# Half-wise state-space results, a setup in 19 beats, a later first batch and a later bonus product in a three-block network kernel

## What is computed

```python
mod = c_act @ w_ada[l] + b_ada[l]
shift, scale, gate = jnp.split(mod, 3, axis=-1)
h = rms_norm(x, norm_g[l]) * (1.0 + scale[:, None, :]) + shift[:, None, :]
u, z_s, q, k, v, z_a = jnp.split(h @ w_in[l], splits, axis=-1)
y_s = s5_mixer(u, ...) * jax.nn.silu(z_s)      # state space, then gelu, then the product with w_glu
y_a = diff_attention(rope(q), rope(k), v, ...) * jax.nn.silu(z_a)
x = x + gate[:, None, :] * (jnp.concatenate([y_s, y_a], axis=-1) @ w_out[l])
```

```python
kk = normalised(k * k_k);  k = k * (1 + (a - 1) * k_a)
y = group_norm(rwkv7_scan(r, decay, k, v, kk, a))
bonus = jnp.sum(r * k * r_k, axis=-1, keepdims=True) * v
return (y + bonus) * g
```

## Time and profile before

| | us |
|---|---|
| median of 3 runs (3295.13 to 3302.15) | 3297.18 |
| the profiled execution | 3302.57 |
| its span in the trace | 3300.5 |
| PE busy | 3008.8 (91%) |
| PE weight loads busy | 2777.6 (84%) |
| DVE busy | 2265.7 (69%) |
| ACT busy | 1621.3 (49%) |
| POOL busy | 324.4 (10%) |

### The profile page before, as it was taken

One profiled execution on the slowest core, in us unless ns is written; L12 is line 12 of the kernel. 1 busy time (PEld: TensorE's weight loads), 2 busy tenths in 40 slices (PEclk: granted clock), 3 DMA queues, 4 the chain that ended last, 5 costly groups with the idle time before them and its releaser, 6 DMA issues.

```text
span 3300.5 us, 60057 instructions
## 1 busy us (share of the span) xinstructions
PE 3008.8 (91%) x24264; PEld 2777.6 (84%) x24264; DVE 2265.7 (69%) x3538; ACT 1621.3 (49%) x2407; POOL 324.4 (10%) x569
## 2 busy tenths in 40 slices
...
GB/s 379 287 243 225 203 209 223 253 198 208 162 155 137 139 147 167 176 179 183 89 112 92 100 108 90 173 130 198 128 171 190 179 192 180 179 187 170 180 147 122
DMA packets 110708, 576.94 MB, mean 175 GB/s; under 512 B 33056, under 2 KB 33088, under 8 KB 46688
## 3 DMA queue, kind: packets, MB, share of 16 engines
...
q10 hardware_dynamic: 576, 3.47, 0.3%
...
## 4 chain that ended last, share of the span: by engine, by line
PE 60%; DVE 24%; ACT 6%; DMA 5%; issue 3%; SPq 1%; POOL 1%; DVEq 0%; ACTq 0%; POOLq 0%
PE acc L911 59%; DVE arena L871 7%; DVE rounded L871 6%; DVE arena L881 3%; ACT arena L908 2%; DVE upper L871 2%; DMA arena<-in_w_ada 2%; ACT rounded L908 2%; DMA arena<-in_w_in 1%; DVE upper L881 1%; ACT upper L908 1%; PE acc L914 1%; SPq L867 1%; DVE rounded L881 1%; DVE arena L877 1%
## 5 line engine op out<-in xcount | busy, mean ns | idle before, releaser
L911 PE MATMUL acc<-rounded 128*128 128x256 f32 x14688 | 1937.1, 291 | 52.6 <-issue 30.4
L911 PEld LDWEIGHTS acc<-rounded 128*128 128x128 f32 x14688 | 1843.6, 196 | 136.1 <-issue 100.3
L871 DVE TENSOR_TENSOR rounded<-arena,rounded 128x1024 fp32r<-128x1024 f32 (+1 forms) x832 | 1005.3, 1208 | 338.8 <-ACT rounded L908 271.0
L908 ACT ACTIVATE rounded<-arena 128x1024 fp32r<-128x1024 f32 (+1 forms) x864 | 883.6, 1023 | 648.7 <-PE acc L911 489.1
L911 PEld LDWEIGHTS acc<-upper_rounded,rounded 128*128 128x128 f32 x4560 | 565.3, 197 | 45.0 <-DVE rounded L871 22.8
L911 PE MATMUL acc<-upper_rounded,rounded 128*128 128x256 f32 x4560 | 573.1, 289 | 23.1 <-DVE rounded L871 20.7
L908 ACT ACTIVATE arena<-arena 128x256 f32<-128x256 f32 (+4 forms) x477 | 253.0, 530 | 306.0 <-DVE arena L871 213.9
L911 PE MATMUL acc<-arena 128*32 128x512 f32 (+8 forms) x1878 | 267.1, 467 | 79.9 <-DMA arena<-in_w_ada 42.7
L871 DVE TENSOR_TENSOR arena<-arena 128x256 f32<-128x256 f32 (+6 forms) x519 | 273.2, 526 | 51.7 <-ACT arena L908 30.1
L911 PEld LDWEIGHTS acc<-arena 128*32 128x32 f32 (+4 forms) x1878 | 122.8, 139 | 143.9 <-DMA arena<-in_w_ada 67.2
L871 DVE TENSOR_TENSOR arena<-acc,arena 128x256 f32<-128x256 f32 (+3 forms) x280 | 119.1, 425 | 178.0 <-PE acc L911 160.3
...
## 6 DMA issues: line engine op xcount, KB each, us to landing
arena<-in_w_in SPq DMA_DIRECT2D x164, 1024.0 KB, 5.0
arena<-in_w_ada SPq DMA_DIRECT2D x88, 1024.0 KB, 5.3
arena<-in_w_up SPq DMA_DIRECT2D x88, 1024.0 KB, 4.8
arena<-in_w_down SPq DMA_DIRECT2D x44, 1024.0 KB, 4.7
arena<-in_w_outa SPq DMA_DIRECT2D x16, 1024.0 KB, 7.3
arena<-in_w_glu SPq DMA_DIRECT2D x16, 1024.0 KB, 5.4
arena<-in_w_outm SPq DMA_DIRECT2D x16, 1024.0 KB, 5.0
arena<-in_w_out SPq DMA_DIRECT2D x16, 1024.0 KB, 4.8
```

Of the source, the lines that this page charges most:

```text
L871: return self.put(self.e and self.e.tensor_tensor(o, a, b, op))
L908: return self.put(self.e and self.e.activation(o, a, f, scale=scale, **kw))
L911: return self.put(self.e and self.e.matmul(o, l, r, start=start, stop=stop, skip_group_check=True))
```

## The change

1. Calls before batch 0: six more in each layer.
2. The results of the state space go out by halves. A new generator `s5_back` waits for batches 7 and 15; for each half it plays `s5_y` (eight writes of half the size), after 14 calls `s5_yr` (POOL waits for them and reads back), after 8 calls the four tiles, each in two beats (`s5_out` with part 0 and 1) three calls apart, and then `part`, 8 calls a tile. The gelu's buffer is a single one, `GS`.
3. `s5_setup` is played in 19 beats. In layer 0 these stay within the same calls as before; in layer 1 each beat has two calls.
4. The recurrent mixer's bonus operand goes to `D2` in place of `RT2`. TensorE's product with it, DVE's product with `v`, the temporary slot and POOL's store belong to step 3, ACT's bias to step 4, and DVE forms `LD` for the exponentials in step 2.
5. `QR`, `QI` (and `SN`) move to the other memory, `XT` to a spare piece of the constants; `upper` grows by 128 columns.

```diff
-IM, QR, QI, R8, ARE, AIM, STP, RE, TH, T1, T2, CO, SI, EM1 = (_c.alloc(64) for _ in range(14))
+IM, R8, ARE, AIM, STP, RE, TH, T1, T2, CO, SI, EM1 = (_c.alloc(64) for _ in range(12))
 P1, P2, PK = (_c.alloc(576) for _ in range(3))
-BC0, BB = _c.alloc(512), _c.alloc(128)
+BC0, GS = _c.alloc(512), _c.alloc(256)
...
+QR, QI = _c.alloc(64), _c.alloc(64)
 KB, VB, PQ = VT_, VT_ + 512, VT_ + 1024
-XT, YT, SN = BB, SI, QR
+XT, YT, SN = CON + CCOL["spare"], SI, QR
...
     def s5(self, l):
-        for i in range(8):
-            self.add("s5_setup", l, i)
-            yield
-            if l:
-                yield
+        for i, parts in enumerate((1, 2, 1, 4, 3, 2, 1, 5)):
+            for part in range(parts):
+                self.add("s5_setup", l, i, part)
+                if l or part == parts - 1:
+                    yield
+                if l:
+                    yield
         self.add("s5_first", l)
         for x in self.s5_prepare(l, 0):
             yield
         for x in self.s5_phases(l, 0):
             yield
         while ("u8", l, 0) not in self.marks:
+            yield
+        for _ in range(6):
             yield
         for b in range(16):
             both = [self.s5_follow(l, b)] + ([self.s5_prepare(l, b + 1)] if b < 15 else [])
...
                     if next(g, self) is self:
                         both.remove(g)
                 yield
-        self.add("s5_y", l)
-        for _ in range(20):
-            yield
-        for j in range(9):
-            self.add("s5_out", l, j)
-            yield
-            yield
-            if j:
-                self.add("part", ("ys", l), j - 1)
-            yield
-            yield
+            self.marks.add(("s5", l, b))
+    def s5_back(self, l):
+        for half in range(2):
+            while ("s5", l, 8 * half + 7) not in self.marks:
+                yield
+            self.add("s5_y", l, half)
+            for _ in range(14):
+                yield
+            self.add("s5_yr", l, half)
+            for _ in range(8):
+                yield
+            for j in range(4 * half, 4 * half + 4):
+                self.add("s5_out", l, j, 0)
+                for _ in range(3):
+                    yield
+                self.add("s5_out", l, j, 1)
+                for _ in range(2):
+                    yield
+                self.add("part", ("ys", l), j)
+                for _ in range(3):
+                    yield
...
-                slot = self.take("rw") if s in (1, 2) else None
+                slot = self.take("rw") if s in (1, 3) else None
...
-                self.bgs += [g5, gm]
+                gy = self.s5_back(0)
+                self.bgs += [g5, gy, gm]
...
-            self.drain(g5)
+            self.drain(g5, gy)
-                g5 = self.s5(1)
-                self.bgs.append(g5)
+                g5, gy = self.s5(1), self.s5_back(1)
+                self.bgs += [g5, gy]
...
-        if s == 2:
+        if s == 3:
             pe.wait_ge("rw_act", ("ld", i))
             pe.wait_ge("rw_dve", ("rk", i))
-            pe.mm(B(4, 0, 256), con("blk"), V(RT2, 256), True, True).then_inc("rw_pe", ("rk", i))
+            pe.mm(B(4, 0, 256), con("blk"), V(D2, 256), True, True).then_inc("rw_pe", ("rk", i))
...
-    def s5_out(l, j):
-        if j < 8:
-            s = TM + 256 * (j % 2)
+    def s5_out(l, j, part):
+        if part == 0:
             act.wait_ge("s5_dve", ("gelu", l, j))
-            act.act(V(s, 256), V(s, 256), ACT.Tanh).then_inc("s5_act", ("gelu", l, j))
+            act.act(V(GS, 256), V(GS, 256), ACT.Tanh).then_inc("s5_act", ("gelu", l, j))
 
...
-        if s == 2:
+        if s == 3:
             bonus[i] = V(TMP + 256 * slot[0], 256)
-        if s == 3:
             act.wait_ge("rw_dve", ("ld2", i))
             act.act(V(RT1, 256), V(CU, 256), ACT.Exp)
             act.act(V(RT2, 256), V(CU, 256), ACT.Exp, scale=-1.0)
             act.act(V(LD, 256), V(LD, 256), ACT.Exp).then_inc("rw_act", ("ex", i))
+        if s == 4:
+            act.wait_ge("rw_dve", ("bo", i))
             act.act(bonus[i], bonus[i], ACT.Identity, bias=par("lnx_b", i)).then_inc("rw_act", ("bo", i))
-        if s == 4:
             act.wait_ge("rw_pe", ("tab", i))
             act.act(V(Q0T, (384, 2), (192, 2), (1, 64)), B(7, 0, (64, 2), (128, 2), (1, 64)), ACT.Copy)
...
+        if i == 3 and part == 0:
             dve.wait_ge("s5_act", ("pk", l))
             dve.copy(V(R8, 64), V(PK + 8, (9, 64)))
             dve.wait_ge("s5_act", ("tanh", l))
             dve.ts(V(T1, 64), V(EM1, 64), -1.0, 1.0, MUL, ADD)
             dve.recip(V(T1, 64), V(T1, 64))
             dve.stt(V(EM1, 64), V(EM1, 64), 2.0, V(T1, 64), MUL, MUL)
-            sin_arg(V(P1, 576), V(TM, 576), V(CC1, 576), con("ph1"), con("ph1r")).then_inc("s5_dve", ("p", l, 0))
-        if i == 4:
-            sin_arg(V(P2, 576), V(TM, 576), V(CC1, 576), con("ph2"), con("ph2r")).then_inc("s5_dve", ("p", l, 1))
-        if i == 5:
+        if i == 3 and part == 1:
+            turns_of(V(CC1, 576), V(TM, 576), con("ph1"))
+        if i == 3 and part == 2:
+            turned(V(P1, 576), V(TM, 576), V(CC1, 576))
+        if i == 3 and part == 3:
+            bounded(V(P1, 576), con("ph1r")).then_inc("s5_dve", ("p", l, 0))
+        if i == 4 and part == 0:
+            turns_of(V(CC1, 576), V(TM, 576), con("ph2"))
+        if i == 4 and part == 1:
+            turned(V(P2, 576), V(TM, 576), V(CC1, 576))
+        if i == 4 and part == 2:
+            bounded(V(P2, 576), con("ph2r")).then_inc("s5_dve", ("p", l, 1))
+        if i == 5 and part == 0:
             sin_arg(V(CO, 64), V(IM, 64), V(T1, 64), 0.25, con("hpi")).then_inc("s5_dve", ("trig", l, 0))
+        if i == 5 and part == 1:
             sin_arg(V(SI, 64), V(IM, 64), V(T1, 64), 0.0, con("zero")).then_inc("s5_dve", ("trig", l, 1))
             dve.ts(V(T2, 64), V(IM, 64), 0.5, None, MUL).then_inc("s5_dve", ("trig", l, 2))
...
-    def s5_out(l, j):
-        if j:
-            i = j - 1
-            s, y = V(TM + 256 * (i % 2), 256), V(U8 + 256 * i, 256)
-        if j < 8:
-            if j == 0:
-                dve.wait_ge("s5_yt", l)
-            yj, sj = V(U8 + 256 * j, 256), V(TM + 256 * (j % 2), 256)
-            dve.stt(yj, V(UT + 256 * j, 256), par("ssm_d", l * 8 + j), yj, MUL, ADD)
+    def s5_out(l, j, part):
+        yj, sj, uj = V(U8 + 256 * j, 256), V(GS, 256), V(UT + 256 * j, 256)
+        if part == 0:
+            dve.wait_ge("s5_yt", (l, j // 4))
+            dve.stt(yj, uj, par("ssm_d", l * 8 + j), yj, MUL, ADD)
             dve.tt(sj, yj, yj, MUL)
             dve.ts(sj, sj, 0.044715 * GELU_C, GELU_C, MUL, ADD)
             dve.tt(sj, sj, yj, MUL).then_inc("s5_dve", ("gelu", l, j))
-        if j:
-            dve.wait_ge("s5_act", ("gelu", l, i))
-            dve.stt(V(UT + 256 * i, 256), s, 1.0, y, ADD, MUL).then_inc("s5_dve", ("out", l, i))
+        else:
+            dve.wait_ge("s5_act", ("gelu", l, j))
+            dve.stt(uj, sj, 1.0, yj, ADD, MUL).then_inc("s5_dve", ("out", l, j))
 
     def att(l, h, i):
         if i == 1:
...
-            dve.stt(V(RT2, 256), V(Rf, 256), par("r_k", i), V(Kf, 256), MUL, MUL).then_inc("rw_dve", ("rk", i))
+            dve.stt(V(D2, 256), V(Rf, 256), par("r_k", i), V(Kf, 256), MUL, MUL).then_inc("rw_dve", ("rk", i))
+            dve.tt(V(LD, 256), V(CU, 256), V(LD, 256), SUB).then_inc("rw_dve", ("ld2", i))
+        if s == 3:
             t = tile_ready(dve, slot)
             dve.wait_ge("rw_pe", ("rk", i))
             dve.tt(V(t, 256), B(4, 0, 256), V(Vf, 256), MUL).then_inc("rw_dve", ("bo", i))
-        if s == 3:
-            dve.tt(V(LD, 256), V(CU, 256), V(LD, 256), SUB).then_inc("rw_dve", ("ld2", i))
             dve.wait_ge("rw_act", ("ex", i))
             dve.tt(V(Rf, 256), V(Rf, 256), V(RT1, 256), MUL)
...
-    def s5_y(l):
-        pool.wait_ge("s5_act", ("y", l, 15))
+    def s5_y(l, half):
+        pool.wait_ge("s5_act", ("y", l, 8 * half + 7))
         for q in range(8):
-            dst = bass.AP(tensor=m.scr_y.tensor, offset=m.scr_y.offset + l * 262144 + q * 32,
-                          ap=[[256, 16], [4096, 64], [1, 32]])
-            pool.dma(dst, V(U8, 64, 32, p0=16 * q, np_=16), "s5_y8", (l, q))
-        pool.wait_ge("s5_y8", (l, 7))
-        pool.dma(V(U8, 8, 256), m.scr_y[l].rearrange("(j p) t -> p j t", p=128), "s5_yt", l)
+            dst = bass.AP(tensor=m.scr_y.tensor, offset=m.scr_y.offset + l * 262144 + half * 131072 + q * 32,
+                          ap=[[256, 16], [4096, 32], [1, 32]])
+            pool.dma(dst, V(U8 + 1024 * half, 32, 32, p0=16 * q, np_=16), f"s5_y8{half}", (l, q))
+    def s5_yr(l, half):
+        pool.wait_ge(f"s5_y8{half}", (l, 7))
+        src = m.scr_y[l, 512 * half:512 * half + 512].rearrange("(j p) t -> p j t", p=128)
+        pool.dma(V(U8 + 1024 * half, 4, 256), src, "s5_yt", (l, half))
...
     def rw(i, s, slot):
-        if s in (1, 2):
```

(5 more changed lines are left out.)

46 lines of the change are left out of this document (29 added, 17 removed).

## The result

The changed kernel's median is 3269.02 us (3267.48 to 3272.13, four runs), the kernel before beside it 3296.15; the ratio is 0.9916, 95% interval 0.9898 to 0.9933. It is faster by 27 us where 57 were forecast. The profiled execution took 3272.13 us with a span of 3270.3, against 3302.57 and 3300.5.

A forecast was written before the change was run, and what follows sets the result against it. The prediction saw TensorE held up in the slow stages by VectorE's work, DMA round trips and weight fetches. Its terms summed to -57.5 us, 3245 for the profiled execution; with the median 5.4 lower it gave 3240, range 3214 to 3272.

The forecast's parts named there:

- The first halves in `w_in`: Second part of `w_in`: the first half's write, read-back and four tiles cost 10 us in layer 1, 6 in layer 0.
- that alone I count as nothing: All later batches lie 12 blocks later; counted as no cost, within 3 us either way a layer.
- the rest is largely the small gaps of 496 instructions: Layer 1's second part of `w_in`: how VectorE's time outside its 291.4 busy of 355.8 us was explained.
- VectorE full with double the price: Rival, `w_in`: VectorE is full, so the added work costs 32 us instead of 16, total 3256; 12%.
- the other seven terms: Forecasts outside `w_in`'s second parts: first parts -6, -7; `w_outa` -15, -19.5; `w_glu` -16; `w_outm` +3.5; recurrent mixer -13.5.
- Bonus: Recurrent mixer: bonus product one step later gains 13.5 us, 10.5 from its eight waits and 3 from the following step.
- Setup: Layer 1's setup in 19 beats: layer 0's `w_glu` gains 16 us, its `w_outm` loses 3.5.
- `w_outa`: Results by halves: layer 1 falls to 49.4 us, gain 19.5; layer 0 to some 65, gain 15.
- a half as dear as the whole: Rival, `w_outa`: half a copy costs as much as a whole, 6.5 us more in each layer, total 3253; 6%.
- Delay: First parts of `w_in`: first batch six calls later shortens waits for rearranged input, gaining 7 us (layer 1) and 6 (layer 0).
- The slower rival: Rival, `w_in`: VectorE stands for the first half's read-back; 35 us late in each layer gives +12.5, total 3310; 4%.

The follow-up runs named there:

- e14: e3 with plain VectorE filler, 11.6 us a layer, at the blocks of the first half's tiles in `w_in`; 3269.76 us, ratio 0.9924.
- e15: e14 with about half of the filler work, 6.2 us a layer; 3258.6 us, ratio 0.9896.
- e3: Changed kernel with all eight output tiles in `w_outa`, the first half still written and read back in `w_in`; 3242.82 us, ratio 0.9851.
- e12: Changed kernel with the four VectorE instructions ahead of each tile's tanh issued one by one, 2 blocks apart; 3268.22 us, ratio 0.9908.
- e1: Changed kernel with the six-call delay before the first batch taken out; 3267.69 us, ratio 0.9927.
- e10: e3 with the six-call delay before the first batch taken out; 3251.56 us, ratio 0.987.
- e8: Kernel before with the six-call delay before the first batch alone; 3297.28 us, ratio 1.0009.
- e7: Kernel before with the bonus product's step and buffer changed and nothing else; 3280.81 us, ratio 0.9956.
- e5: Changed kernel with layer 1's setup back in 8 beats, all within layer 0's `w_glu`; 3276.3 us, ratio 0.9949.
- e9: e3 with layer 1's first phase step moved from layer 0's `w_outm` to the first part of layer 1's `w_in`; 3240.6 us, ratio 0.9828.
- e2: Changed kernel with the whole state-space result written, read back and finished after the last batch; 3254.94 us, ratio 0.9879.

## Why the prediction was right in sign and wrong in size

**The step that failed** is the term "The first halves in `w_in`", 10 + 6 us, and with it "that alone I count as nothing" for the shift of the batches. Measured: 43.3 us. Three things are in it.
- I named the work rightly, 4 x 2.8 = 11.2 us of VectorE a layer, and then let a part of it hide, all the more in layer 0, because VectorE was busy 71% of the stage there and 82% in layer 1. No part hides (e14, e15: 1.05 to 1.17 us per us); layer 0, with its 293.0 of 414.7 us busy, pays as much as layer 1. With the price of 1.1 the term is 25 us for both layers. That "the rest is largely the small gaps of 496 instructions" was a misreading besides: of the 64.4 us in which VectorE is not busy in that stage, 35.4 are waits, for ScalarE most of all. They were no slack either.
- The tiles in the changed kernel cost more than plain work: 29.2 us in their own blocks against e3, for 21.2 us more of VectorE's time, where plain work at 1.1 would have cost 23. e12 excludes the burst. The 3.23 us in each layer in which VectorE stands for ScalarE's half of a finished tile are as large as the difference; that they are its cause is argued, not tested. By the medians of e1, e3 and e10 tiles and shift cost some 10 us more together than apart, and most of that is not located.
- The shift of 12 blocks costs 8.4 us in the first 248 blocks of layer 1's second part, at the same amount of work (8.9 in e8, same stretches); in layer 0 it is not to be told from 0 (-3.1 in e8, +3.8 from e10 to e3). The forecast allowed 3.

These make some 39 of the 43.3 us. The remaining 4 are within what one reading of these stages differs from another.

The added condition "wrong if `w_in` grows by more than 30 in all" was met by the second parts, with 43.3; with the first parts, which got 17.7 shorter, `w_in` grew by 25.6. The rival that named it, VectorE full with double the price, had the right cause and, at 32, still too small a size; it had 12%. That the other seven terms came within 5 us is the merit of the reading by stages; that their errors and the rest cancel to nothing is luck.

**What held.** Bonus: -16.6, by the edit alone -15.4 (e7), against -13.5. The eight waits for the bonus operand became five, 11.8 us in e7, against "under 13". The waits of the step after didn't all go: one of 5.3 us stands at block 104, for another VectorE result, which before had no wait of its own there. (The sum that gave 10.5 is, done again, 22.6 - 12.6 + 0.9 = 10.9.)
Setup: -17.0 and +8.0 by e5 against -16 and +3.5. The mechanism in `w_outm` (phase step ahead of the closing norm) is 3.5 us by e9, my whole term; the other 4.5 are the pieces moved in, VectorE 55.1 instead of 44.3 us busy in a stage of 58, which I had counted as covered.
`w_outa`: 46.9 and 65.5 us against 49.4 and 65, with no wait of VectorE on a read-back. Pool's timeline in layer 1, changed kernel:
```profile
1247.61 5.00 POOL L885 DMA_DIRECT2D scr_y<-upper  x8 [3.80 <-ACT upper L926]
1255.57 0.78 POOL L885 DMA_DIRECT2D upper<-scr_y  x1 [2.96 <-DMA scr_y<-upper]
```
7.96 us from first write to read-back, where the whole took 16.75 and I had taken 10: in layer 1 half cost half. In layer 0 it was 11.26 of 17.62 (616.98 to 628.24, before 601.70 to 619.32), in e3 8.1 in both layers. The rule of the Trainium skill (DMA: Bandwidth & Descriptors, Measured) says that transfers under 64 KB are dominated by their descriptors; the price that my rival had drawn from it, a half as dear as the whole, is not what the traces show for these writes of 64 KB instead of 128. VectorE comes to the tile at 1266.33. But the gain isn't that of the early first half alone: e2, with all of the result behind the last batch, has 56.7 us in layer 1, 12.2 under before, of which 4.5 go again in `w_glu` (50.6 against 46.1).
Delay: -9.5 and -8.2 in the first parts, against -6 and -7; the queue behind the input reads in layer 0 showed as a wait of TensorE of 3.4 us for modulation weights, where 2.5 of the 8.6 us were to be lost.
The slower rival didn't come up: no wait on the first half's read-back.

**The balance.** Bonus -15.4 (e7) and setup -9.0 (e5) make -24 of the measured -27 us (by medians -14.6 and -7.3, so -22). Delay and halves together bring next to nothing: what they gain in `w_outa` and at the head of `w_in` they give back in the body of `w_in`. Left in `w_outa`, the tiles bring another 26 us (e3), and with the phase step moved 3240.6 us (e9).
